# Order of the matmuls in four projections: one PSUM bank after another instead of four banks in turn

## The chip, the cores and the metric

The kernel runs on one core of a Trainium2 chip. The metric is the device time of one execution in microseconds (us).

## What is computed

One inference step of a two-layer decoder, for a prompt of 1,024 tokens and a group of 8 x 8 sample tokens with the same weights, 1,088 tokens in all, everything in float32:

```
h  = x
h  = h + retention(rmsnorm(h))     # proj = h @ w_in  (1024 x 6144), chunked recurrence, gate, @ w_out (2048 x 1024)
h  = h + ssd(rmsnorm(h))           # proj = h @ w_in  (1024 x 6176), conv, chunked recurrence, gate, @ w_out (2048 x 1024)
y  = rmsnorm(h)
```

The outputs are y for both groups and the new recurrent and convolution states. The four products with large weights are the projections p1 (retention in), p2 (retention out), p3 (SSD in, 6,144 of its columns) and p4 (SSD out).

## The kernel before

The phases follow each other: `phase_input` turns x so that features lie on the partitions; `phase_project` with tag p1; `phase_retention`; p2; `phase_norm_steps` (norm of layer 2 and its small product for the time steps); p3; `phase_ssd`; p4; `phase_output`.

**A projection.** Its output features are cut into tiles of 128 (48 in p1, 48 in p3, 8 each in p2 and p4). The 1,088 tokens are cut into `BLK` = 4 blocks of `TB` = 272. The product of a tile takes K row tiles of 128 inputs (K = 8 in p1 and p3, 16 in p2 and p4). Operands are split in two parts in the format fp32r: the weights into `whi` and `wlo`, the activations into `hi` and `lo`. Three passes are added up: whi with hi, whi with lo, wlo with hi. A tile is thus K x 3 x 4 matmuls, 96 in p1 and p3, 192 in p2 and p4.

**PSUM.** `acc_ps` has two halves `s` of four banks; block b of a tile is summed up in bank b of its half, in its first 272 columns. While TensorE fills one half, ACT and DVE empty the other, always after the last matmul of the tile (`mm_done`), and set the half free with `ps_free`.

**Who does what.** SP loads weight tile n+2 once tile n's weights are split (`lo_done`), and stores results. ACT splits off `whi` (L376; L382 for the first tile, in four parts), DVE makes `wlo` (L524; L531 for the first tile, in four parts, each announced by `first_lo`). The split of tile n+2 is asked for when the matmuls of tile n are done. For p1 the normalised input is made during the first tile: `norm_parts` gives one row tile k of hi and lo after another (DVE L226 the scaled row, ACT L197 hi, L170 lo, on DVE for even and on POOL for odd k), and TensorE waits for each with `norm.ready(pe, k)`. The sums of squares for the norm are the matmuls of L204. On DVE the split of the second tile (L535) stands ahead of `norm.norms` (L537).

**Other lines that the prediction uses.** In the retention, L839 and L842 add up r_y, whose four column ranges of 128 all lie in one bank: per range two records of L839 (one call) and four of L842 (two calls). L827 writes two banks, one call each. The calls with plain float32 operands leave two records each; the calls of L471, in fp32r, one each.

Of the kernel before, what the change touches and what calls it, by code (L numbers as in the profile page):

```python
# [17 lines left out]
BLK = 4  # L18
# [69 lines left out]
def dma_wait(eng, sem, n):  # L88

    eng.wait_ge(sem, 16 * n)  # L90
# [147 lines left out]
def phase_project(nc, sb, ps, sem, tag, K, w, segments, hi, lo, out, A, resid=None, params=None, O=None,  # L238
                  norm=None, keep=None):
# [9 lines left out]
    with ExitStack() as ctx:  # L249
# [20 lines left out]
        if norm:  # L270
            norm = norm_parts(nc, sb, ps, sem, ctx, *norm, A, hi, lo)
# [5 lines left out]
        parts = [slice(i * K // 4, (i + 1) * K // 4) for i in range(4)]  # L277
        first_in = [sem(f"{tag}first_in{i}") for i in range(4)]
        first_hi, first_lo = sem(tag + "first_hi"), sem(tag + "first_lo")
# [24 lines left out]
        def loop(eng, body):  # L304

            for a, b, kind in segments:
                us, ue = a // 2, b // 2
                if us == 0:
                    body(0, True, ue == 1 and b == n_tiles, kind)
                    us = 1  # L310
                end = ue - 1 if b == n_tiles else ue
                if end > us:
                    with eng.Fori(us, end) as u:
                        body(u, False, False, kind)
                if b == n_tiles and ue - 1 >= us:
                    body(ue - 1, False, True, kind)

        with nc.Block() as block:
# [135 lines left out]
            @block.tensor  # L454
            def _(pe):
                def body(u, first, last, kind):
                    for s in range(2):
                        n = 2 * u + s
                        if not (first and s == 0):
                            pe.wait_ge(lo_done, n + 1)  # L460
                        if not first:
                            pe.wait_ge(ps_free, n - 1)
                        passes = ((whi, hi), (whi, lo), (wlo, hi))
                        for k in range(K):
                            if first and s == 0 and k % (K // len(parts)) == 0:
                                pe.wait_ge(first_lo, k // (K // len(parts)) + 1)
                            if norm and first and s == 0:
                                norm.ready(pe, k)
                            for j, (wt, x) in enumerate(passes):
                                for b in range(BLK):  # L470
                                    mm = nc.tensor.matmul(  # L471
                                        acc_ps[:, s, b, 0:TB], wt[:, s, k, :], x[:, k, b * TB:(b + 1) * TB],
                                        start=(k == 0 and j == 0), stop=(k == K - 1 and j == 2))
                        mm.then_inc(mm_done, 1)
                if norm:
                    norm.sums(pe, total)
                loop(pe, body)
                if "conv" in kinds:

                    dma_wait(pe, ident_in, 1)  # L480
                    for i in range(CONVDIM // P // BT):
                        pe.wait_ge(ps_free, n_tiles - 1 + i)
                        pe.wait_ge(tails_out, CONVDIM // P * (i + 1) // 2 + B)
                        for k in range(BT):
                            last = nc.tensor.transpose(acc_ps[0:CTAIL, i, k // 4, (k % 4) * P:(k % 4 + 1) * P],
                                                       tails[:, i * BT + k, :], ident[:, :])
                        last.then_inc(tails_turned, 1)
# [1540 lines left out]
```

## Time and profile before

| | |
|---|---|
| two runs | 2574.9 and 2576.28 us, median 2575.59 |
| span of the profiled execution | 2575.9 us; the page gives no time beside it |
| instructions | 46,067 |
| TensorE matmuls (PE) | busy 2294.3 us, 89% |
| TensorE weight loads (PEld) | busy 2075.5 us, 81% |
| DVE, ACT, POOL | busy 40%, 30%, 20% |
| mean granted TensorE clock | 0.934 |

The profile is one execution recorded by the hardware. Times are from the span's start. PE is the matmuls of TensorE, PEld its weight loads, which overlap them; DVE is VectorE, ACT ScalarE, POOL GpSimd, SPq the queue of DMA issues of SyncE. A matmul's record is longer than the time to the next one's start, since several are in flight: the pitch from start to start says what one costs, not the mean duration. L471 is line 471 of the kernel.

### The profile page before, as it was taken

To read this page: it belongs to the slowest core of one execution; us is meant where nothing else is said; L and a number is where in the kernel's file an instruction comes from. 1 tells how busy PE (TensorE), PEld (TensorE's weight loads), DVE (VectorE), ACT (ScalarE), POOL (GpSimd) and SP (SyncE) were. 2 spreads that over 40 slices of the span, in tenths; PEclk is the share of its full clock that TensorE was granted. 3 is DMA by queue.
4 is the path that set the end of the run, shared out by engine and by line. 5 is a ranking of instruction groups with operands and counts; after the bars stand their busy time and mean duration, and the time that the engine had idled before them with its cause. 6 is when DMAs were issued, how large, how long until landed. Compare 5 with 4: busy or idle time off the path is not lost. (4 is left out here: it accounts for less than half of the span.)

```text
span 2575.9 us, 46067 instructions
## 1 busy us (share of the span) xinstructions
PE 2294.3 (89%) x16118; PEld 2075.5 (81%) x16118; DVE 1027.3 (40%) x1513; ACT 784.8 (30%) x1503; POOL 504.6 (20%) x744
## 2 busy tenths in 40 slices
PE   5999999997899998996699999999928777888996
PEld 4999999997555656996499999999926555667995
DVE  4455100211344343110522145555528887883112
ACT  5111111221333332000321134344326666562002
POOL 2222000000344332000200000000016666561000
PEclk8999999999899988998799999999958988888998
DMA  5232322222756654312122222222135666564225
GB/s 191 76 101 69 110 99 84 94 91 71 199 181 194 183 165 140 101 52 78 52 93 94 91 84 92 84 92 92 60 90 147 156 154 146 137 157 129 68 69 165
DMA packets 427452, 291.87 MB, mean 113 GB/s; under 512 B 115856, under 2 KB 388880, under 8 KB 427312
## 3 DMA queue, kind: packets, MB, share of 16 engines
q1 hardware_dynamic: 379560, 262.44, 34.4%
q10 hardware_dynamic: 47808, 28.32, 3.5%
q8 instruction: 52, 0.85, 0.1%
q14 instruction: 32, 0.26, 0.0%
HBM read 190.50 MB, written 100.20 MB: 113 GB/s over the span
## 5 line engine op out<-in xcount | busy, mean ns | idle before, releaser
L471 PE MATMUL p1acc_ps<-xn1hi,p1whi 128*128 128x272 f32 x1536 | 256.2, 289 | 12.0 <-DVE xn1lo L170 7.8
L471 PE MATMUL p3acc_ps<-xn2hi,p3whi 128*128 128x272 f32 x1536 | 256.4, 289 | 3.9 <-DVE p3wlo L531 3.9
L471 PE MATMUL p3acc_ps<-xn2lo,p3whi 128*128 128x272 f32 x1536 | 256.3, 289 | 0.0
L471 PE MATMUL p3acc_ps<-xn2hi,p3wlo 128*128 128x272 f32 x1536 | 255.9, 288 | 0.0
L471 PE MATMUL p1acc_ps<-xn1lo,p1whi 128*128 128x272 f32 x1536 | 255.5, 288 | 0.0
L471 PE MATMUL p1acc_ps<-xn1hi,p1wlo 128*128 128x272 f32 x1536 | 255.3, 288 | 0.0
L471 PEld LDWEIGHTS p1acc_ps<-xn1hi,p1whi 128*128 128x128 f32 x1536 | 216.3, 188 | 13.9 <-issue 8.6
L471 PEld LDWEIGHTS p3acc_ps<-xn2hi,p3whi 128*128 128x128 f32 x1536 | 218.1, 189 | 4.7 <-DVE p3wlo L531 4.7
L471 PEld LDWEIGHTS p3acc_ps<-xn2lo,p3whi 128*128 128x128 f32 x1536 | 218.2, 189 | 0.0
L471 PEld LDWEIGHTS p3acc_ps<-xn2hi,p3wlo 128*128 128x128 f32 x1536 | 217.9, 188 | 0.0
L471 PEld LDWEIGHTS p1acc_ps<-xn1lo,p1whi 128*128 128x128 f32 x1536 | 216.7, 189 | 0.0
L471 PEld LDWEIGHTS p1acc_ps<-xn1hi,p1wlo 128*128 128x128 f32 x1536 | 216.5, 188 | 0.0
L524 DVE TENSOR_TENSOR p1wlo<-p1raw,p1whi 128x1024 fp32r<-128x1024 f32 x47 | 57.6, 1225 | 398.2 <-ACT p1whi L376 398.1
L376 ACT ACTIVATE p1whi<-p1raw 128x1024 fp32r<-128x1024 f32 x47 | 49.8, 1060 | 373.3 <-PE p1acc_ps L471 373.1
L557 DVE SCALAR_TENSOR_TENSOR p3acc<-p3mid,params,p3acc 128x1024 f32<-128x1024 f32 x96 | 123.3, 1285 | 74.1 <-ACT p3acc L410 65.3
L524 DVE TENSOR_TENSOR p3wlo<-p3raw,p3whi 128x1024 fp32r<-128x1024 f32 x47 | 57.6, 1225 | 215.7 <-ACT p3whi L376 215.7
L376 ACT ACTIVATE p3whi<-p3raw 128x1024 fp32r<-128x1024 f32 x47 | 49.8, 1060 | 229.6 <-PE p3acc_ps L471 227.4
L471 PE MATMUL p2acc_ps<-g1hi,p2whi 128*128 128x272 f32 x512 | 85.8, 290 | 7.5 <-DVE p2wlo L531 7.5
L471 PE MATMUL p4acc_ps<-g2hi,p4whi 128*128 128x272 f32 x512 | 86.2, 290 | 6.8 <-DVE p4wlo L531 6.8
L471 PE MATMUL p4acc_ps<-g2lo,p4whi 128*128 128x272 f32 x512 | 85.7, 289 | 0.0
L471 PE MATMUL p4acc_ps<-g2hi,p4wlo 128*128 128x272 f32 x512 | 85.6, 289 | 0.0
L471 PE MATMUL p2acc_ps<-g1lo,p2whi 128*128 128x272 f32 x512 | 85.3, 288 | 0.0
(287 smaller groups left out, 4110.7 us busy)
## 6 DMA issues: line engine op xcount, KB each, us to landing
ret_proj<-p1res SPq DMA_DIRECT2D x48, 544.0 KB, 4.9
ssd_proj<-p3res SPq DMA_DIRECT2D x48, 544.0 KB, 2.7
p1raw<-in_ret_w_in SPq DMA_DIRECT2D x47, 512.0 KB, 4.5
p3raw<-in_ssm_w_in SPq DMA_DIRECT2D x47, 512.0 KB, 3.8
r_vg<-ret_proj SPq DMA_DIRECT2D x64, 256.0 KB, 3.4
r_sin<-in_state_ret SPq DMA_DIRECT2D x32, 512.0 KB, 4.4
out_ret_sample<-r_sout ACTq DMA_DIRECT2D x32, 512.0 KB, 4.1
s_zx<-ssd_proj SPq DMA_DIRECT2D x128, 128.0 KB, 2.3
```

The lines of the kernel that those rows point to most:

```text
L376: nc.scalar.activation(whi[:, s, :, :], raw[:, s, :, :], ACT.Copy).then_inc(hi_done, 1)
L471: mm = nc.tensor.matmul(acc_ps[:, s, b, 0:TB], wt[:, s, k, :], x[:, k, b * TB:(b + 1) * TB], start=(k == 0 and j == 0), stop=(k == K - 1 a ...
L524: nc.vector.tensor_tensor(wlo[:, s, :, :], raw[:, s, :, :], whi[:, s, :, :], ALU.subtract).then_inc(lo_done, 1)
L557: nc.vector.scalar_tensor_tensor(ap, xp[:, w:w + SEQ], wc, ap, ALU.mult, ALU.add)
```

## The change

In the TensorE program of `phase_project` the loop over the four token blocks moves from the innermost place to the outermost. Before, for each row tile k and each pass, the four blocks (banks) followed each other with the same stationary tile. Now block 0 takes all K x 3 contributions, then block 1, and so on. The waits of the first tile (`first_lo`, `norm.ready`) stand in block 0 alone. The matmuls themselves, their start and stop flags and the increment of `mm_done` behind the last one are the same.

```diff
-                        for k in range(K):
-                            if first and s == 0 and k % (K // len(parts)) == 0:
-                                pe.wait_ge(first_lo, k // (K // len(parts)) + 1)
-                            if norm and first and s == 0:
-                                norm.ready(pe, k)
-                            for j, (wt, x) in enumerate(passes):
-                                for b in range(BLK):
+                        for b in range(BLK):
+                            for k in range(K):
+                                if first and s == 0 and b == 0 and k % (K // len(parts)) == 0:
+                                    pe.wait_ge(first_lo, k // (K // len(parts)) + 1)
+                                if norm and first and s == 0 and b == 0:
+                                    norm.ready(pe, k)
+                                for j, (wt, x) in enumerate(passes):
                                     mm = nc.tensor.matmul(
                                         acc_ps[:, s, b, 0:TB], wt[:, s, k, :], x[:, k, b * TB:(b + 1) * TB],
                                         start=(k == 0 and j == 0), stop=(k == K - 1 and j == 2))
```

## Rows read from the trace of the kernel before

**Rows 1.** The page: span, and TensorE's busy tenths in 40 slices

```profile
span 2575.9 us, 46067 instructions
...
PE   5999999997899998996699999999928777888996
```

**Rows 2.** Groups of instructions: busy us, mean ns, then idle before

```profile
L471 PE MATMUL p1acc_ps<-xn1hi,p1whi 128*128 128x272 f32 x1536 | 256.2, 289 | 12.0 <-DVE xn1lo L170 7.8
...
L471 PEld LDWEIGHTS p1acc_ps<-xn1hi,p1whi 128*128 128x128 f32 x1536 | 216.3, 188 | 13.9 <-issue 8.6
...
L471 PE MATMUL p2acc_ps<-g1hi,p2whi 128*128 128x272 f32 x512 | 85.8, 290 | 7.5 <-DVE p2wlo L531 7.5
```

**Rows 3.** Table by stretches of the projections

```profile
core 0: us, PE busy (x) PEld busy (x) DVE busy (x) ACT busy (x) POOL busy (x), PEclk, DMA share, GB/s
...
65.30:629.50 564.20, 564.17 (x4514) 563.95 (x4512) 150.95 (x93) 103.47 (x100) 49.08 (x16) 1.00 0.27 88
1008.60:1012.50 3.90, 3.83 (x17) 3.83 (x18) 2.09 (x4) 1.52 (x3) 0.00 (x0) 0.50 0.98 274
1012.50:1202.70 190.20, 190.18 (x1521) 189.96 (x1520) 24.51 (x14) 13.41 (x7) 0.00 (x0) 1.00 0.24 79
1287.60:1292.40 4.80, 4.77 (x21) 4.77 (x22) 1.38 (x4) 2.27 (x4) 0.00 (x0) 0.50 0.82 224
1292.40:1870.00 577.60, 577.60 (x4592) 577.57 (x4592) 254.49 (x280) 182.92 (x249) 16.93 (x94) 1.00 0.26 86
...
2347.20:2538.70 191.50, 191.31 (x1521) 191.09 (x1519) 24.75 (x15) 13.43 (x7) 0.00 (x0) 1.00 0.23 77
```

**Rows 4.** Timeline of TensorE in the retention: start us, us, what

```profile
800.09 1.88 PE L827 MATMUL r_st<-r_v,r_kt 128*128 128x512 f32 x4
801.81 0.39 PE L794 MATMUL r_misc<-r_sq,r_ones 128*128 128x128 f32 x2
802.03 0.39 PE L839 MATMUL r_y<-r_sc,r_v 128*128 128x128 f32 x2
...
804.71 0.61 PE L781 MATMUL r_misc<-r_qk 128*128 128x128 f32 x4
```

**Rows 5.** Timeline of TensorE mid p1, windows opening at different matmuls

```profile
299.19 0.28 PE L471 MATMUL p1acc_ps<-xn1hi,p1wlo 128*128 128x272 f32 x1
299.31 0.66 PE L471 MATMUL p1acc_ps<-xn1hi,p1whi 128*128 128x272 f32 x4
...
299.44 0.54 PE L471 MATMUL p1acc_ps<-xn1hi,p1whi 128*128 128x272 f32 x3
```

**Rows 6.** Timeline, starts of p2 and p3

```profile
1008.67 1.27 PE L471 MATMUL p2acc_ps<-g1hi,p2whi 128*128 128x272 f32 x4 [7.53 <-DVE p2wlo L531]
...
1010.40 1.44 DVE L531 TENSOR_TENSOR p2wlo<-p2raw,p2whi 128x512 fp32r<-128x512 f32 x2 [0.82 <-ACT p2whi L382]
...
1287.63 1.27 PE L471 MATMUL p3acc_ps<-xn2hi,p3whi 128*128 128x272 f32 x4 [3.94 <-DVE p3wlo L531]
...
1288.20 1.26 DVE L531 TENSOR_TENSOR p3wlo<-p3raw,p3whi 128x256 fp32r<-128x256 f32 x3 [0.62 <-ACT p3whi L382]
1288.70 1.11 PE L471 MATMUL p3acc_ps<-xn2lo,p3whi 128*128 128x272 f32 x4
...
1289.61 1.11 PE L471 MATMUL p3acc_ps<-xn2hi,p3wlo 128*128 128x272 f32 x4
```

**Rows 7.** Timeline of TensorE, end of p1's first tile

```profile
61.23 0.74 PE L471 MATMUL p1acc_ps<-xn1hi,p1whi 128*128 128x272 f32 x4 [0.67 <-DVE xn1lo L170]
...
63.70 0.77 PE L471 MATMUL p1acc_ps<-xn1hi,p1whi 128*128 128x272 f32 x4 [0.73 <-POOL xn1lo L170]
...
65.31 0.66 PE L471 MATMUL p1acc_ps<-xn1hi,p1whi 128*128 128x272 f32 x4
```

**Rows 8.** Table by stretches, p1's first tile (columns as in rows 3)

```profile
53.40:56.80 3.40, 3.40 (x17) 3.25 (x16) 3.40 (x4) 1.53 (x2) 1.70 (x1) 0.50 0.00 0
56.80:63.70 6.90, 4.42 (x31) 3.79 (x30) 4.29 (x2) 1.81 (x2) 4.47 (x2) 1.00 0.00 0
```

## The prediction

> **What bounds the kernel now.** I read the page first: TensorE is busy for 89% of the span (the table above), and its slices, 64 us each, stand at 9 tenths or more where the projections lie, the 3rd to the 9th, the 17th to the 19th, the 22nd to the 29th and the 38th and 39th among them [rows 1]. Then the groups of instructions, for what a projection issues: in p1 three forms of 1,536 matmuls on 272 columns each, as many in p3, and three times 512 in p2 and in p4, so 12,288 in all. The reader is to see the count of weight loads beside it: 1,536 LDWEIGHTS for 1,536 matmuls, although each stationary tile is used four times in a row [rows 2]. The weights are loaded anew for every matmul already. Then the table by stretches: outside its first tile, p1 runs 4,514 matmuls in 564.20 us without a gap, 125.0 ns from one to the next; p2 1,521 in 190.20 (125.0), p3 4,592 in 577.60 (125.8), p4 1,521 in 191.50 (125.9 with its edges), all at a granted clock of 1.00, the 2.4 GHz level [rows 3]. DVE, ACT and POOL are busy for 27%, 18% and 9% of the long stretch of p1 (150.95, 103.47 and 49.08 us), so nobody else is near to being late. The projections are bound by this pitch and by how each first tile starts, and what the order of matmuls does to either goes to the end of the kernel in full, since TensorE has no idle time in them that could take it up.
>
> The profile's span is 2575.9 us and the two runs gave 2574.9 and 2576.28, median 2575.59. The page lists no time outside the span, so I add to 2575.9 and take the result as the time; the difference of 0.3 us is nothing here. 2% of it, about what a measurement of this kernel can tell from no change, is 51.5 us.
>
> **What the change leaves alone.** The same 12,288 matmuls with the same operands and one weight load each, the same waits per tile, the same increment on the last matmul of a tile, the same bank half (4 of 8 banks) handed to ACT and DVE at the end of a tile. Nobody reads a single bank early: the evacuations wait for the count of whole tiles, so that three banks are now complete sooner brings nothing. No DMA is moved. The semaphore waits that it moves are only those of a projection's first tile.
>
> **Part 1: the pitch.** Before, consecutive matmuls go to four different banks and three of four weight loads repeat the tile just loaded. After, 23 of 24 (p1, p3) or 47 of 48 (p2, p4) steps stay in one bank and on the same 272 columns, and nearly every load brings another tile (only whi for hi and then for lo repeats). No stretch of the trace has such a stream in this form of matmul, so I bound it by the nearest rows.
>
> Same bank: in the retention, the product r_y is 24 records that all go to one bank, in four runs of six on the same 128 columns each, with other weights from call to call. They start at 802.03 and the next group at 804.71: 2.68 us / 24 = 111.7 ns [rows 4]. In the same view records of 512 columns (L827, four in 1.72 us, two to each of two banks) take 0.43 us, the full-clock cost of two cycles per column; two cycles for 128 columns are 106.7 ns. So all that is not streaming, a penalty for staying in a bank included, is at most 5.0 ns. Between the first record of L794, in another bank, and the first of r_y two records take 802.03 - 801.81 = 0.22 us, 110 ns each: steps that change the bank and steps that stay in it look alike to the rounding. The stream into one bank thus shows an extra cost between 0 and 5.0 ns; I take 0 for that likeness, and keep 5.0 for the slower rival.
>
> Below nothing: the present pitch of 125.0 ns is 11.7 ns over 272 columns at 2.4 GHz (113.3 ns), and no row says what these 11.7 are. If the turn of banks is in them, the change takes it away. The rows with one bank keep 5.0 of it, so a gain is at most 6.7 ns by them (p1, p2) and 7.5 (p3, p4). I take 0: at the half clock two groups of four in p3 start at 1288.70 and 1289.61, 0.91 us apart, 227 ns each, which is 272 columns at 1.2 GHz with nothing left over [rows 6], and the 0.43 us of L827, with its change of bank, is pure streaming as well.
>
> Other weights each time: the step into a new stationary tile is one of every four now. The step into new weights is 299.19 to 299.31, 0.12 us; the next, with the same weights, 299.31 to 299.44, 0.13 us [rows 5]. A new tile costs nothing that the row shows. What the rows do show is that the pitch is 125.0 in two projections and 125.8 in the other two, with the same loop: something in the operands' placement is worth 0.8 ns. The new order pairs them differently, so I give the pitch 0.8 ns to either side: 12,288 x 0.8 = 10 us.
>
> One rule of the Trainium skill speaks against the change: Perfetto Trace Analysis, section Matmul Optimizations, says that all eight PSUM banks should be kept in use for the most instruction-level parallelism. The one-bank rows at 111.7 ns do not agree with a cost in that; by the rule alone the time would go up, which is rival C below, and the page has no figure for it.
>
> **Part 2: first tiles.** In p1 the normalised input arrives row tile by row tile while the first tile runs. The starts of its last two k groups are 61.23 and 63.70, released by DVE's and POOL's L170 [rows 7], and the chain that makes them (DVE, ACT, DVE or POOL) waits for no matmul, so the change does not move them. Before, the 12 matmuls of a k step fill most of the wait for the next: at 63.70 only 12 are left, done at 65.31 [rows 7], 1.61 us. After, the block b=0 takes all the waits with 3 matmuls per step, and at 63.70 there remain 3 + 3 x 24 = 75: 75 x 125.0 = 9.4 us. The difference is 7.8 us, all of it on the path, as TensorE never idles later in p1.
>
> The clock: before, it was 1.00 from 56.8 on, with TensorE busy for 4.42 of 6.90 us, and 0.50 from 53.4 to 56.8 [rows 8]. After, only 3 of 12 matmuls are issued per step until 63.70, about a sixth of the time, less than ahead of any fall in these rows, so I expect the granted clock at 0.50 when the long stream begins. What such a start costs: p2 runs 17 matmuls in its first 3.90 us at 0.50 in place of 31 (17 x 0.125 = 2.1, so 1.8 us lost), p3 21 in 4.80 (2.2 lost) [rows 3]. I take 1.9; it is 0 if the clock holds. Together 9.7 us, between 7.8 and 10.0.
>
> Who waits behind it: the second tile's weights were split before the norm's own work (L535 stands ahead of L537), and the third's are asked for when the first tile is done, with a whole tile of 12 us ahead of them where ACT and DVE need 1.06 and 1.23 us. So nothing else becomes late; all of p1 moves by 9.7 us, and the phases after it with it.
>
> In p2, p3 and p4 the first tile waits for quarters of the weights. In p3 the three later quarters are split from 1288.20 to 1289.46 [rows 6], 0.42 us each. The b=0 block now takes a quarter in 6 matmuls, at the half clock 1.36 us: it wants the second at 1287.63 + 1.36 = 1288.99 (there at 1288.62), the third at 1290.35, the fourth at 1291.71. No wait. In p2 a quarter is 12 matmuls, 2.7 us: wanted at 1011.4, 1014.1 or sooner as the clock rises, the last split ends at 1011.84 [rows 6]. No wait, and p4 has the same shape. Cost 0; if a quarter's DMA is late, up to a microsecond each.
>
> **The sum.** 2575.9 + 0 (pitch) + 9.7 (p1's first tile) + 0 = 2585.6 us.
>
> **The rivals.**
> A, the forecast: 2585.6, own range 2575 to 2596 by the 0.8 ns of pitch. 70%.
> B, the order of operands moves the pitch by 1 to 3 ns, either way: the present spread of single steps (0.12 to 0.13 us) speaks for some such effect, the constant 125.0 against it. 12,288 x 3 = 37 us: 2549 to 2622. 12%, half each way.
> C, slower: adding to the bank that the matmul before is still filling holds each one up. A matmul lasts 289 ns in the record while the next starts after 125, so three are in flight and would now all be bound for one bank. At the bound of 5.0 ns: 12,288 x 5.0 = 61 us, with the 9.7 a time of 2647. It decides the sign from (51.5 - 9.7) / 12,288 = 3.4 ns on. Against it stand the one-bank rows of the retention. 9%.
> D, faster: the change of bank is part of the 11.7 ns. At the bound 6,144 x (6.7 + 7.5) = 87 us off: 2575.9 + 9.7 - 87.2 = 2498. It needs 5.0 ns per matmul to pass 2%. Against it stand the half-clock pitch and L827's 0.43 us. 9%.
> That the change does nothing at all to the first tile of p1 (if the hardware order were another than the program's) would give 2576 and lies in A's range.
>
> **How the numbers follow.** The time is A's. Faster by over 2%: D, 9%. Slower by over 2%: C, 9%. Within: A and B, 82%. The range of 8 in 10 takes A and most of B: 2560 to 2612.
>
> **What would show it.** In the changed kernel's table by stretches the pitch in the middle of p1 and p3: 125.0 and 125.8 by A; 118 by D, 130 by C, the same in all four projections. In p1's first tile groups of 3 matmuls at the present ready times, then 75 in a row from 63.7, the end of that tile near 75.0 in place of 65.31, and a granted clock of 0.50 in that stretch's beginning. First tiles of p2 to p4 as long as now. The prediction is wrong if the pitch moves by more than 1 ns, or if the clock falls at other places than p1's first tile.

## The result, and the profile after

The changed kernel took 2588.66 us (median of 2587.53 and 2589.78) against 2575.59. The ratio on record is 1.0055, 95% interval 1.0037 to 1.0072; it is not the quotient of the two medians, which is 1.0051. The changed kernel is slower, by half a percent: clear of 1, and well under 2%. A later comparison with more runs (the last experiment) gave 1.0045, interval 1.0033 to 1.0057 (quotient of the medians 1.0037).

The page of the changed kernel, span and busy times, beside [rows 1]:

```profile
span 2585.7 us, 46067 instructions
PE 2297.1 (89%) x16118; PEld 2076.2 (80%) x16118; DVE 1027.1 (40%) x1513; ACT 784.8 (30%) x1503; POOL 503.3 (19%) x744
```

As many instructions, as many matmuls and weight loads, and 9.8 us more span. The table by stretches of the changed kernel, beside [rows 3] and [rows 8] (first the columns, then p1's first tile up to its last wait, the rest of that tile in two pieces, the rest of p1, the start of p2, the rest of p3):

```profile
core 0: us, PE busy (x) PEld busy (x) DVE busy (x) ACT busy (x) POOL busy (x), PEclk, DMA share, GB/s
43.50:63.86 20.36, 7.21 (x22) 5.07 (x22) 17.78 (x9) 6.66 (x6) 13.19 (x4) 0.50 0.09 27
63.86:67.20 3.34, 3.34 (x15) 3.34 (x15) 0.00 (x0) 0.00 (x0) 0.00 (x0) 0.50 0.00 0
67.20:74.90 7.70, 7.70 (x63) 7.70 (x63) 0.00 (x0) 0.00 (x0) 0.00 (x0) 0.99 0.01 2
74.90:640.10 565.20, 565.20 (x4514) 565.17 (x4512) 150.83 (x93) 103.48 (x100) 49.01 (x16) 1.00 0.27 87
1017.70:1021.60 3.90, 3.85 (x17) 3.86 (x18) 2.08 (x3) 1.86 (x3) 0.00 (x0) 0.50 0.94 272
1303.10:1877.70 574.60, 574.60 (x4589) 574.60 (x4588) 254.27 (x280) 182.83 (x249) 16.87 (x94) 1.00 0.26 87
```

The timeline of TensorE around the end of that first tile, beside [rows 7]. A merged row of the timeline gives start, duration, and in brackets how long TensorE had waited and for what:

```profile
61.42 0.57 PE L471 MATMUL p1acc_ps<-xn1hi,p1whi 128*128 128x272 f32 x1 [1.40 <-DVE xn1lo L170]
...
63.86 0.59 PE L471 MATMUL p1acc_ps<-xn1hi,p1whi 128*128 128x272 f32 x1 [1.42 <-POOL xn1lo L170]
64.25 0.43 PE L471 MATMUL p1acc_ps<-xn1lo,p1whi 128*128 128x272 f32 x1
...
67.38 0.28 PE L471 MATMUL p1acc_ps<-xn1hi,p1whi 128*128 128x272 f32 x1
...
74.88 0.28 PE L471 MATMUL p1acc_ps<-xn1hi,p1whi 128*128 128x272 f32 x1
```

And the same stretch of the kernel before, from the first matmul of p1 to its last wait:

```profile
43.20:63.70 20.50, 15.00 (x84) 13.51 (x84) 17.89 (x9) 6.67 (x6) 13.33 (x4) 0.83 0.06 18
```

What to see. TensorE is released for the last k step at 63.86, where it was 63.70. In the 20.36 us before that it ran 7 x 3 = 21 matmuls where before it ran 7 x 12 = 84 (the table counts 22, for the one that is released at 63.86 touches the edge), and it waits most of the time: busy for 7.21 us where it was 15.00, at a granted clock of 0.50 where the mean was 0.83. Then 75 matmuls follow, the first 15 at a granted clock of 0.50 (3.34 us, 0.22 us each), and the second tile begins at 74.88. From the last wait to the second tile it is 11.02 us, where it was 65.31 - 63.70 = 1.61. The first tile lasts 74.88 - 43.51 = 31.4 us in place of 22.1, 9.3 us more. After it the pitch is 565.20 / 4,512 = 125.3 ns in p1 (125.0 before, [rows 3]) and 574.60 / 4,587 = 125.3 ns in p3 (125.8 before); two matmuls of each count had begun ahead of the stretch. From the second tile to the last matmul those are +1.3 and -2.5 us. p2 starts at the half clock with 17 matmuls in 3.90 us, exactly as before.

So in the two profiled executions the difference of 9.8 us is nearly all p1's first tile. The rest of the phases moved by 1 to 2 us either way: between the last matmul of p1 and the first of p2 lay 379.5 us before and 377.7 after, between p3 and p4 473.6 and 475.4. Such gaps move without any change too: between p1 and p2 a second profile of the kernel before (the last but one group of experiments) has 375.5 us, 4.0 less than the first. So the close fit of one profile with the other is in part luck, and the shares have to come from the experiments.

### The profile page after: what moved, and what is told of

The parts are those of the page before. It is cut to its first block and busy times, and to the rows that moved or that the text cites. A ratio compares the mean times of both kernels' runs of the same rounds, so it can differ in the third digit from the quotient of the medians.

```text
span 2585.7 us, 46067 instructions
## 1 busy us (share of the span) xinstructions
PE 2297.1 (89%) x16118; PEld 2076.2 (80%) x16118; DVE 1027.1 (40%) x1513; ACT 784.8 (30%) x1503; POOL 503.3 (19%) x744
## 5 line engine op out<-in xcount | busy, mean ns | idle before, releaser
L471 PE MATMUL p1acc_ps<-xn1hi,p1whi 128*128 128x272 f32 x1536 | 444.0, 289 | 19.6 <-DVE xn1lo L170 10.7
L471 PE MATMUL p3acc_ps<-xn2hi,p3whi 128*128 128x272 f32 x1536 | 442.3, 288 | 4.2 <-DVE p3wlo L531 4.2
L471 PE MATMUL p1acc_ps<-xn1lo,p1whi 128*128 128x272 f32 x1536 | 444.7, 290 | 0.0
L471 PE MATMUL p1acc_ps<-xn1hi,p1wlo 128*128 128x272 f32 x1536 | 444.1, 289 | 0.0
L471 PE MATMUL p3acc_ps<-xn2lo,p3whi 128*128 128x272 f32 x1536 | 443.9, 289 | 0.0
L471 PE MATMUL p3acc_ps<-xn2hi,p3wlo 128*128 128x272 f32 x1536 | 443.3, 289 | 0.0
L471 PEld LDWEIGHTS p1acc_ps<-xn1hi,p1whi 128*128 128x128 f32 x1536 | 290.6, 189 | 22.2 <-issue 12.0
L471 PEld LDWEIGHTS p1acc_ps<-xn1lo,p1whi 128*128 128x128 f32 x1536 | 290.6, 189 | 0.0
L471 PEld LDWEIGHTS p1acc_ps<-xn1hi,p1wlo 128*128 128x128 f32 x1536 | 290.6, 189 | 0.0
L471 PE MATMUL p2acc_ps<-g1hi,p2wlo 128*128 128x272 f32 x512 | 148.6, 290 | 0.0
```

What stands on the lines that cost most here:

```text
L471: mm = nc.tensor.matmul(acc_ps[:, s, b, 0:TB], wt[:, s, k, :], x[:, k, b * TB:(b + 1) * TB], start=(k == 0 and j == 0), stop=(k == K - 1 a ...
```

## The experiments

The theory: the banks do not matter, and the loss is p1's first tile, in part work that piles up behind the last wait, in part a lower clock. The code cuts below show the lines that matter; "..." stands for what is left out. The rivals: the pitch pays for the bank or for the order in all tiles.

**Undo the change in the first tiles.**

```diff
+ blocks_outside = not (first and s == 0)      # the old order for each projection's first tile
...
```

> Block after block as in the change, but the first tile of every projection keeps the old order (four banks in turn). First-tile theory: the whole difference of the change sits in p1's first tile, so p1's first tile lasts 22.1 us again, the span is 2574.8 us (before less 1.1 us for the pitch), ratio to before 0.9996. Pitch theory (the changed order costs something in the later 111 tiles that the profile of one execution does not show): ratio 1.003 or more, 2584 us or more.

Measured: ratio 1.0014, interval 1.0003 to 1.0025. The loss falls to between a quarter and a third of the changed kernel's (1.0055 and 1.0045); the first tile lasts 22.1 us again (42.97 to 65.10). Both forecasts were missed: the interval holds neither the first tile's 0.9996 nor the pitch theory's 1.003. Something of 1 to 6 us remains in the later tiles, and the profile shows what it is. The table by stretches of this kernel, p1 after its first tile and the middle of p3:

```profile
66.00:631.00 565.00, 565.00 (x4503) 565.00 (x4502) 150.99 (x93) 102.79 (x100) 49.11 (x16) 1.00 0.27 87
1350.00:1700.00 350.00, 350.00 (x2790) 350.00 (x2789) 147.44 (x160) 106.97 (x144) 9.42 (x52) 1.00 0.27 89
```

565.00 / 4,501 and 350.00 / 2,788 are 125.5 to 125.6 ns. The later tiles have the same order as in the changed kernel and yet not its 125.3: I come back to that.

**The change in p1's first tile alone.**

```diff
+ blocks_outside = bool(norm) and first and s == 0      # the new order for this tile only
...
```

> The old order everywhere, block after block in p1's first tile alone. First-tile theory: that tile lasts 31.4 us in place of 22.1, the pitch stays 125.0 and 125.8 ns, time 2585 us, ratio 1.0036. Pitch theory: within 3 us of before, ratio 1.001 or less.

Measured: ratio 1.0037, interval 1.0024 to 1.0050, as forecast. The first tile lasts 31.5 us (44.10 to 75.63). One of the 112 tiles carries the greater part of the change's loss. But the pitch of p3 was 125.0 and not 125.8, with the old order and the operands where they were:

```profile
1350.00:1700.00 350.00, 350.00 (x2803) 350.00 (x2802) 144.19 (x155) 105.58 (x143) 8.81 (x49) 1.00 0.27 90
```

**One bank, the old order of operands.**

```diff
- acc_ps[:, s, b, 0:TB], wt[:, s, k, :], x[:, k, b * TB:(b + 1) * TB],
+ own = k == K - 1 and j == 2 and b > 0      # the last three of a tile
...
+ acc_ps[:, s, b if own else 0, 0:TB], wt[:, s, k, :], x[:, k, b * TB:(b + 1) * TB],
+ start=own or (k == 0 and j == 0 and b == 0), ...
```

> The kernel before with its order of operands, but all matmuls of a tile except the last three add into bank 0 (the other banks get only their last contribution, so the projections' values are not the reference's). It changes the bank alone. If banks do not matter: 125.0 ns per matmul in p1 and 125.8 in p3 as before, 2576 us. If staying in a bank costs (rival C): up to 130 ns, 2637 us. If the change of banks was part of the 11.7 ns (rival D): down to 118 ns, 2489 us.

**Banks in turn, the new order of operands.**

```diff
- acc_ps[:, s, b, 0:TB], wt[:, s, k, :], x[:, k, b * TB:(b + 1) * TB],
+ acc_ps[:, s, (3 * k + j) % BLK, 0:TB], wt[:, s, k, :], x[:, k, b * TB:(b + 1) * TB],
...
```

> The changed kernel with its order of operands (block after block), but each matmul adds into the next bank in turn, so blocks are mixed and the projections' values are not the reference's. It changes the bank alone on the other side. If the operands' order sets the small shift of the pitch: 125.3 ns in p1 and p3 and 125.5 in p2 and p4 as in the changed kernel, 2586 us. If the bank sets it: 125.0 in p1 and 125.8 in p3.

Measured: 2576.0 and 2582.08 us, one run each; 2576 and 2586 were forecast. The tables by stretches (100 to 600 us lies in p1, 1350 to 1700 in p3), first the one-bank kernel:

```profile
100.00:600.00 500.00, 500.00 (x4002) 500.00 (x4001) 134.00 (x83) 94.23 (x91) 42.93 (x14) 1.00 0.27 90
...
1350.00:1700.00 350.00, 350.00 (x2784) 350.00 (x2783) 147.11 (x161) 106.37 (x144) 9.35 (x52) 1.00 0.27 90
```

Then the kernel with banks in turn:

```profile
100.00:600.00 500.00, 500.00 (x3993) 500.00 (x3992) 133.03 (x83) 93.02 (x90) 42.85 (x14) 1.00 0.29 94
...
1350.00:1700.00 350.00, 350.00 (x2797) 350.00 (x2796) 142.21 (x155) 105.43 (x142) 9.37 (x52) 1.00 0.27 90
```

And the changed kernel itself:

```profile
100.00:600.00 500.00, 500.00 (x3993) 500.00 (x3992) 132.69 (x82) 92.22 (x90) 42.87 (x14) 1.00 0.29 94
1350.00:1700.00 350.00, 350.00 (x2796) 350.00 (x2796) 143.98 (x155) 104.74 (x141) 8.84 (x49) 1.00 0.27 90
```

Take 2 or 3 off each count for matmuls that began ahead of the stretch. The one-bank kernel has 125.0 and 125.8, the values of before, with 93 or 189 of every 96 or 192 matmuls of a tile in one bank; the kernel with banks in turn has 125.3 and 125.3, the values of the changed kernel, with another bank at every matmul. The bank is worth nothing for the pitch, to 0.1 ns. Rivals C and D have fallen, and so has, for this kernel, the rule of the Trainium skill on using all banks (Perfetto Trace Analysis, Matmul Optimizations), as far as it would be about the pitch. All these kernels keep the two halves of four banks, one filled while the other is emptied; what that is worth no run here shows. The order of operands, or what comes with it in the program, is worth some tenths of a nanosecond.

**Keep the clock up while waiting.**

```diff
+ if norm and first and s == 0 and b == 0 and k < K - 1:
+     for i in range(9):
+         nc.tensor.matmul(acc_ps[:, s, 3, 0:TB], whi[:, s, k, :], hi[:, k, 0:TB], start=True, stop=True)
...
```

> The changed kernel with nine more matmuls after each of the first seven k steps of p1's first block, in the time in which TensorE waits for the normalised input (they write the fourth bank, which is written anew later). The work after the last wait is the same 75 matmuls. If 1.5 to 1.9 us of the loss are the lower clock at the start of the long stream: its granted clock is 1.00, and the first tile ends 9.4 us after the last wait in place of 11, 29.8 us for the tile in place of 31.4. If the clock has no part: 31.4 us as in the changed kernel.

Measured, table by stretches of this kernel, up to the last wait and from there to the second tile:

```profile
45.40:65.90 20.50, 14.88 (x84) 13.51 (x84) 17.89 (x9) 6.68 (x6) 13.34 (x4) 0.84 0.05 15
65.90:75.40 9.50, 9.48 (x75) 9.49 (x76) 0.00 (x0) 0.00 (x0) 0.00 (x0) 1.00 0.01 2
```

The 75 matmuls take 9.5 us at a granted clock of 1.00, where the changed kernel took 11.0: the clock's part is 1.5 us. The rows of the changed kernel give the same: 15 matmuls at 0.22 us in place of 0.125 are 1.5 us. The tile lasts 30.0 us (45.40 to 75.43; 29.8 was forecast). Its time was 2586.02 us in a single run, against 2571.32 in the single run of before on that chip; runs of before alone lie up to 11 us apart, so this pair can't show the 1.5 us, the trace does. Of the 9.3 us, 1.5 are thus clock, and 7.8 are 63 matmuls of 125 ns that used to run in the waits.

**What the pitch is made of.**

```diff
+ cols = TB if k == 0 and j == 0 else 240      # in the second kernel 128
- acc_ps[:, s, b, 0:TB], wt[:, s, k, :], x[:, k, b * TB:(b + 1) * TB],
+ acc_ps[:, s, b, 0:cols], wt[:, s, k, :], x[:, k, b * TB:b * TB + cols],
```

> The kernel before with 240 in place of 272 columns in all matmuls of a tile but the first four (32 columns of each block get only their first contribution, so values are not the reference's). It asks what the pitch of 125.0 ns is made of. If each load and matmul takes a fixed time to issue and streaming lies beneath it: still 125.0 ns, 2576 us. If 11.7 ns come on top of the streaming: 100.0 + 11.7 = 111.7 ns, 12,176 matmuls x 13.3 ns less, 2414 us.

> As with 240 columns, but with 128 (the other columns get only their first contribution). Fixed time to issue: still 125.0 ns, 2576 us. Streaming plus 11.7 ns: 65 ns, 1840 us or more.

```diff
- for b in range(BLK):
-     ... acc_ps[:, s, b, 0:TB], wt[:, s, k, :], x[:, k, b * TB:(b + 1) * TB]
+ for b in range(3):
+     ... acc_ps[:, s, b, 0:362], wt[:, s, k, :], x[:, k, b * 363:b * 363 + 362]
...
+ mm = nc.tensor.matmul(acc_ps[:, s, 3, 0:TB], ...)      # once per tile
```

> The kernel before with three blocks of 362 columns per stationary tile in three banks and one more matmul per tile into the fourth bank (blocks lie otherwise in the banks than the evacuation takes them, so values are not the reference's); 73 matmuls per tile in p1 and p3, 145 in p2 and p4. Fixed time to issue with streaming beneath: 362 columns stream in 150.8 ns and the pitch is 151 to 154 ns, a tile of p1 takes 11.0 to 11.2 us in place of 12.0, 2460 to 2485 us. Streaming plus 11.7 ns: 162.5 ns, a tile takes 11.85 us, 2560 us.

Measured: 2425.04, 3654.68 and 2581.43 us against 2571.32 for before on that chip. Tables by stretches, 240 columns (p3):

```profile
1350.00:1700.00 350.00, 350.00 (x3100) 350.00 (x3100) 201.91 (x230) 142.54 (x203) 15.45 (x85) 1.00 0.31 100
```

128 columns (p1):

```profile
100.00:600.00 500.00, 500.00 (x2340) 500.00 (x2340) 96.99 (x53) 48.57 (x48) 42.54 (x14) 0.50 0.17 55
```

362 columns (p1, p3):

```profile
100.00:600.00 500.00, 500.00 (x3050) 500.00 (x3050) 134.09 (x83) 94.23 (x91) 43.04 (x14) 1.00 0.28 91
...
1350.00:1700.00 350.00, 350.00 (x2083) 350.00 (x2082) 144.61 (x158) 103.44 (x140) 9.36 (x52) 1.00 0.27 88
```

That 125.0 ns are a fixed time to issue a load and its matmul has fallen: with 240 columns the pitch is 350 / 3,097 = 113.0 ns, 13.0 above the streaming at 2.4 GHz; with 272 it is 11.7 above, with 362 it is 164.1 and 168.3 ns, 13.3 and 17.5 above. (These are means over a tile, in which 4 of 96 or 1 of 73 matmuls have 272 columns.) So between 240 and 362 columns, at the full clock, something of 12 to 18 ns comes on top of the streaming; what it is stays open. The forecasts by that theory were low all the same: 111.7 ns and 2414 us, 162.5 ns and 2560 us. Three larger blocks gain nothing in p1, 73 x 164.1 ns = 11.98 us per tile against 12.00, and lose in p3, 73 x 168.3 = 12.3 us.

At 128 columns both forecasts failed: 213.9 ns, at a granted clock of 0.50 for the whole projection although TensorE is busy for 500 of 500 us. Why the clock stays down is open. The clock alone does not explain the pitch either: at the same half clock 272 columns take 227 ns [rows 6] and 128 columns nearly as much. That looks like a lowest time for a load with its matmul. By an estimate from these rows, 213.9 ns at 1.2 GHz would be 107 ns at 2.4 GHz, below the 113.0 of 240 columns, so the longer matmuls do not speak against it; no run here tests it.

**Why 125.0 here and 125.8 there.**

```diff
...
+ for _ in range(1):              # in the second kernel 8
+     pe.wait_ge(first_lo, 1)
  loop(pe, body)
```

> The kernel before once more, unchanged, for its pitch alone. If the pitch of each projection belongs to the program: 125.0 ns in p1 and p2, 125.8 in p3 and p4 again. If each execution falls into one or the other: any of the two, in any projection.

> The kernel before with one more instruction on TensorE ahead of each projection's first tile, a wait that is already met or about to be; operands, banks and order are untouched. If the pitch hangs on where the instructions lie, it changes in at least one projection (125.8 to 125.0 in p3, or the reverse in p1). If it hangs on the operands' places or on the order, it stays 125.0, 125.0, 125.8, 125.8.

> As with one wait more, but with eight: a shift by eight instructions. If the place of the instructions counts, a third pattern of pitches; if operands' places or order count, 125.0, 125.0, 125.8, 125.8.

The first of the three is the kernel before, unchanged. Measured: 2570.35, 2574.15 and 2574.74 us, one run each. The middle of p3 in the three, one table by stretches each, first before again:

```profile
1350.00:1700.00 350.00, 350.00 (x2802) 350.00 (x2802) 147.54 (x161) 108.46 (x147) 9.97 (x55) 1.00 0.28 91
```

One wait more:

```profile
1350.00:1700.00 350.00, 350.00 (x2784) 350.00 (x2783) 146.93 (x160) 106.97 (x146) 9.40 (x52) 1.00 0.27 90
```

Eight waits more:

```profile
1350.00:1700.00 350.00, 350.00 (x2802) 350.00 (x2802) 148.33 (x161) 108.54 (x147) 9.38 (x52) 1.00 0.27 90
```

The same program that had 125.8 ns in p3 now has 125.0. The pitch of the old order is not a property of the program or of the operands' places: in p3 and p4 each execution falls into one of two values. In all profiles of kernels with 272 columns, from the first matmul of the second tile to the last:

```
pitch, ns                     p1      p2      p3      p4
before                        125.0   125.0   125.8   125.8
before again                  125.0   125.0   125.0   125.0
new order in p1's first tile  125.0   125.0   125.0   125.0
one bank, old operands        125.0   125.0   125.8   125.8
one wait more                 125.0   125.0   125.8   125.0
eight waits more              125.0   125.0   125.0   125.8
changed kernel                125.3   125.5   125.3   125.5
changed kernel again          125.3   125.5   125.3   125.5
banks in turn, new operands   125.3   125.5   125.3   125.5
changed, with fillers         125.3   125.5   125.3   125.5
new order but first tiles     125.6   125.5   125.6   125.5
```

In p3 the old order's two values are 3.8 us apart, in p4 1.1 us. Of the 7.3 us between the two profiled spans of before (2575.9 and 2568.6) these are 4.9, so part of the spread of before's runs (2568.91 to 2580.32 in the last comparison) may well be this; it was profiled in two executions only. In p1 and p2 all six profiles of the old order have 125.0 and all five of the new one 125.3 to 125.6, so there the order, or what comes with it, does cost 0.3 to 0.6 ns. The new order had one pair of values in four profiles and another in the one with the old first tiles. What sets the values, and whether the waits moved anything, these runs don't tell.

**The changed kernel again.**

> The changed kernel once more, against before on the same chip. From p1's first tile 9.3 us and from the pitch -1.1 us: 8.2 us or ratio 1.0032; from the first two runs 13.1 us or 1.0051. The pitch in the profile 125.3 ns in p1 and p3, 125.5 in p2 and p4 again.

Measured: 2585.39 us, median of 6, against 2575.88, median of 11; ratio 1.0045, interval 1.0033 to 1.0057, which takes in 1.0051 and 1.0055, and of the forecast's parts the sum with the pitch of before at its lower value: 9.3 + 0.28 x 4,512 (p1) + 0.28 x 4,512 (p3) + 0.47 x 1,344 x 2 (p2, p4) = 9.3 + 3.8 = 13.1 us; with before in its upper values in p3 and p4 it is 8.2 us (1.0032), just below the interval. The two halves of the change, measured alone on one chip, give 1.0037 (p1's first tile) and 1.0014 (all the others), together 1.0051, within the interval too. So the loss is 9.3 to 9.5 us of first tile (22.1 us in the profiles of before, 31.4 and 31.5 in those of the new order) and, by the pitch, between -1 and 4 us of the rest.

No version that computes the same in another order beats the kernel before: the changed kernel with the old first tiles comes nearest, at 1.0014.

## Why the prediction was right

**The pitch, taken as unchanged.** Right in size: 125.3 and 125.5 ns, within the 0.8 ns allowed to either side. The bound for one bank, 0 to 5.0 ns from the retention's r_y, was resolved at 0 by the two kernels that changed the bank alone, and so was the possible gain of 6.7 ns. The reason given for the 0.8 ns, the operands' placement, failed: the pitch went from 125.8 to 125.0 in an execution of the same program.

**The p1 first tile.** The working held term by term: the last wait ended at 63.86 (63.70 forecast), 75 matmuls behind it, 7.8 us of them new. The clock's share was forecast at 1.9 and came out at 1.5 (11.0 against 9.5 us with the fillers), since the clock was back after 15 matmuls in 3.34 us and not after 3.9 or more as at the starts of p2 and p3. The tile ends at 74.88; 75.0 was forecast.

**The first tiles of p2 to p4, cost 0.** Right for their starts: in p2 17 matmuls in the first 3.90 us, as before. From first matmul to second tile p2 took 26.6 us after and 25.8 before, but 26.1 in the kernel that changed p1 alone and 26.1 in the second profile of the changed kernel, so the 0.7 us are no more than what two executions differ by.

**What was left out.** Time outside the span: I took none for want of it on the page, while every later run has its time and its span side by side, 2576.0 and 2574.2, 2570.35 and 2568.6, 2587.53 and 2585.7, 1.8 us apart. Added to the sum of 2585.6 it would be 2587.4, nearer to the 2588.66, but then the starting value, 2575.9 and 1.8, is 2.1 us above the median of before. The plainer comparison is that of the change: 9.7 us forecast, 13.1 between the medians of two runs each and 9.5 between those of the last comparison. What the first tile does not explain is within what the old order's two pitches move.

**Luck.** The sum, 2585.6, meets the profiled span, 2585.7, to 0.1 us. The terms do not fit that well: the clock came 0.4 us cheaper, the pitch moved p1 by +1.3 us and p3 by -2.5, and the two phases between projections moved by -1.7 and +1.7. They happened to cancel. Against the lower pitch of before the same change would have read 3.8 us more than the first tile, where the prediction had put nothing.

**The rivals.** B did not come about: in the table no projection moved by 1 ns. C and D did not either, for the reason that was held against them: rows of one bank and rows of changing banks had looked alike.

## What to carry to other kernels

Where a stationary tile is loaded anew for every matmul, as it is here, the order of the matmuls within a tile hardly changes the steady pitch (by 0.8 ns of 125 at most here), and staying in one PSUM bank doesn't change it. What the order changes is the start: put the loop over inputs that still arrive outermost and let each arrival feed all the work it can, for what is not done in the waits stands behind the last one, and here it began at 1.2 GHz. Look for such a price first in the one tile that waits for its input, then in the other 111.

## What the runs showed of the hardware that was not expected

- The old order has two pitches in p3 and p4, 125.0 and 125.8 ns, and a projection keeps one of them throughout (p3: 350 us with 2,802 matmuls in one execution, 2,784 in another of the same program).
- At the full clock a matmul of 272 columns in fp32r costs 11.7 or 12.5 ns over its streaming, one of 240 13.0 (p3), one of 362 13.3 (p1) or 17.5 (p3), as means over a stretch.
- With 128 columns per matmul and a weight load each, the pitch is 213.9 ns and the granted clock stays at 0.50 for a whole projection, with TensorE busy all the time (500 of 500 us in p1): 1.7 times the time of 272 columns for less than half of the work.
